# Two-layer MoE trunk: a second home for one down weight, down loads later in the queue, one modulation vector in the arena, and a reordered routing

## What is computed

```python
mod = cs @ w_mod[i] + b_mod[i]
sh_m, sc_m, g_m, sh_f, sc_f, g_f = jnp.split(mod, 6, axis=-1)
...
g_sel = jnp.argmax(g_logits, axis=-1)
p_g = jnp.take_along_axis(g_prob, g_sel[:, None], axis=1)
...
top_val, top_idx = lax.top_k(e_in_group, TOP_K_IN_GROUP)
gate = p_g * jax.nn.softmax(top_val, axis=-1)
...
hg = jnp.einsum('sd,edf->sef', t, w_gate)
hu = jnp.einsum('sd,edf->sef', t, w_up)
act = jax.nn.silu(hg) * hu * combine[:, :, None].astype(t.dtype)
return jnp.einsum('sef,efd->sd', act, w_down)
```

## Time and profile before

| what | value |
|---|---|
| median of three executions | 725.58 us (724.47 to 726.06) |
| profiled execution, its own time | 724.7 us |
| span of that execution | 722.6 us |
| HBM read | 268.16 MB, 373 GB/s over the span |
| TensorE busy | 642.3 us (89%), 4266 matmuls |
| VectorE busy | 365.6 us (51%) |
| ScalarE busy | 173.2 us (24%) |

### The profile page before, as it was taken

The page is one execution under the profiler, slowest core; times in us unless marked ns, Lnnn a source line. Parts: engine busy times, 40 slices in busy tenths (PEclk is TensorE's granted clock), DMA queues, the critical chain, the costliest instruction groups (busy, mean ns, idle before and its releaser), DMA issues.

```text
span 722.6 us, 11521 instructions
## 1 busy us (share of the span) xinstructions
PE 642.3 (89%) x4266; PEld 387.3 (54%) x4266; DVE 365.6 (51%) x894; ACT 173.2 (24%) x368; POOL 24.9 (3%) x54
## 2 busy tenths in 40 slices
PE   2699999999998899898998899999889899889994
PEld 1487667467654454454544457575445554545542
DVE  1259876988354334433344388563443334433345
ACT  2113343032322111221112143232122111221123
POOL 5100400000000000000000000000000000000000
PEclk9999999998999999999999999799999999999998
DMA  8999973995579999999999999987999999999991
GB/s 334 353 405 392 335 294 136 411 421 221 233 290 422 420 422 421 422 423 421 422 422 422 416 397 409 362 339 302 422 421 421 422 422 421 423 423 422 421 382 58
DMA packets 49677, 269.61 MB, mean 373 GB/s; under 512 B 3796, under 2 KB 5908, under 8 KB 25072
## 3 DMA queue, kind: packets, MB, share of 16 engines
q1 hardware_dynamic: 48864, 268.22, 91.7%
q0 software_dynamic: 784, 1.00, 0.5%
HBM read 268.16 MB, written 1.05 MB: 373 GB/s over the span
## 4 chain that ended last, share of the span: by engine, by line
PE 49%; DMA 38%; DVE 5%; SPq 5%; issue 2%; ACT 1%; POOL 0%; POOLq 0%; ACTq 0%; DVEq 0%
DMA ring<-in_w_up 33%; PE bank L902 9%; PE bank L881 9%; PE bank L916 5%; PE bank L758 4%; PE bank L607 4%; DMA early_w<-in_w_in 3%; PE bank L869 2%; PE bank L832 2%; PE bank L682 2%; PE bank L692 2%; PE bank L533 2%; DMA dn_w<-in_w_down 2%; PE bank L647 1%; SPq L350 1%
## 5 line engine op out<-in xcount | busy, mean ns | idle before, releaser
L881 PE MATMUL bank<-ring,arena 128*64 128x256 f32 x1024 | 117.3, 382 | 28.4 <-DMA ring<-in_w_up 28.4
L869 PE MATMUL bank<-ring,arena 128*64 128x256 f32 x1024 | 117.6, 382 | 12.6 <-DMA ring<-in_w_gate 12.6
L1178 ACT CAST xn_parts<-arena 128x512 fp32r<-128x512 f32 x64 | 39.6, 618 | 304.9 <-DVE arena L1652 304.9
L881 PEld LDWEIGHTS bank<-ring,arena 128*64 128x64 f32 x1024 | 71.2, 137 | 73.4 <-DMA ring<-in_w_up 40.2
L902 PE MATMUL bank<-dn_w,hT 128*64 128x512 f32 x480 | 109.5, 598 | 0.8 <-DMA dn_w<-in_w_down 0.8
L869 PEld LDWEIGHTS bank<-ring,arena 128*64 128x64 f32 x1024 | 81.0, 137 | 41.6 <-issue 17.6
L1627 DVE SCALAR_TENSOR_TENSOR hT<-hT,bank 128x256 f32<-128x256 f32 x32 | 19.8, 618 | 119.9 <-PE bank L881 119.9
L916 PE MATMUL bank<-xn_parts,sel 128*128 128x512 f32 x256 | 67.1, 405 | 0.0
L902 PEld LDWEIGHTS bank<-dn_w,hT 128*64 128x64 f32 x480 | 32.0, 136 | 62.6 <-issue 60.7
L1652 DVE SCALAR_TENSOR_TENSOR arena<-bank,hT,gates 128x512 f32<-128x512 f32 x64 | 47.9, 749 | 23.9 <-PE bank L902 23.9
L916 PEld LDWEIGHTS bank<-xn_parts,sel 128*128 128x128 f32 x256 | 45.7, 188 | 21.0 <-issue 12.4
(11 more groups left out here) (287 smaller groups left out, 683.7 us busy)
## 6 DMA issues: line engine op xcount, KB each, us to landing
ring<-in_w_gate SPq DMA_DIRECT2D x32, 2048.0 KB, 13.7
ring<-in_w_up SPq DMA_DIRECT2D x32, 2048.0 KB, 18.1
dn_w<-in_w_down SPq DMA_DIRECT2D x30, 2048.0 KB, 10.3
ring<-in_w_mod SPq DMA_DIRECT2D x21, 2048.0 KB, 18.5
ring<-in_w_in SPq DMA_DIRECT2D x2, 2048.0 KB, 22.7
arena<-in_w_mod SPq DMA_DIRECT2D x2, 2048.0 KB, 19.3
ring<-in_w_down SPq DMA_DIRECT2D x2, 2048.0 KB, 14.5
early_w<-in_w_in SPq DMA_DIRECT2D x1, 2048.0 KB, 21.1
```

The lines of the kernel that those rows point to most:

```text
L869: ins = pe.matmul(bank[2][h * WIN:(h + 1) * WIN, 0:FE], xw[:, b, h, k, :], w[:, h, 0, k, :], start=(k == 0), stop=(k == KT - 1))
L881: ins = pe.matmul(bank[3][h * WIN:(h + 1) * WIN, 0:FE], xw[:, b, h, k, :], w[:, h, 1, k, :], start=(k == 0), stop=(k == KT - 1))
L1178: act.copy(xn_parts[:, 0, b, at], y_s[:, b, at]).then_inc(e["y_hi"], 1)
```

## The change

It has four parts. (1) In layer 0, down(1) gets a room of its own, `second_down`: one expert in `xn`, the other in `gates[:, 2:4]`, in two loads of 1 MB, issued behind down(0). (2) SP's first passes are written out: gate(3) and up(3) stand ahead of the down load, and down loads follow later; the loop is turned so that it issues down(p-2), gate(p), up(p). (3) The vector (1,5) is loaded into the arena, not into ring slots 3 and 2; gate(1) and up(1) of layer 1 no longer wait for chunk 23, and the store of `xgT` does. (4) In the routing the matmuls for the totals come first and into a bank of their own; offsets are added by TensorE in PSUM by accumulation, in place of copies and an add on DVE; the six small operations for the two gates of a token move behind the gather; the turning of these gates into rows (`rows_of((gate1, gate2), 7)`) moves behind the first gate product; in layer 1 only half of (1,5) stands ahead of the totals; in layer 0 three of the eight fold matmuls stand between the two halves of the transposes.

```diff
+        second_down = (xn[:, :, :], gates[:, 2:4, :])
         middle = [(m, slot) for m, slot in zip(halves((1, 2)) + halves((1, 4)) + halves((1, 3)) + halves((1, 5)),
-                                               (1, 0, 3, 2, 0, 1, 3, 2))]
+                                               (1, 0, 3, 2, 0, 1, ARENA_A, ARENA_B))]
...
-                else:
-                    sp.wait_ge(S["chunk_done"], chunk_no["mod", 23] + 1)
                 gate_load(l, 1, 2)
                 up_load(l, 1, 2)
...
                 down(l, 0)
+                if l == 0:
+                    sp.wait_ge(S["reduced"], len(reduced))
+                    for half in range(2):
+                        sp.dma_start(second_down[half].rearrange("p t d -> p (t d)"),
+                                     w_down[l][2 + half].rearrange("(p t) d -> p (t d)", t=FT)).then_inc(second_in, 16)
...
-                with sp.Fori(1, groups) as i:
+                gate_next(2, 0, 4), up_next(2, 0, 4), gate_next(3, 1, 6), up_next(3, 1, 6)
+                if l == 0:
+                    sp.wait_ge(E[l]["down_done"], 2)
+                    down(l, 4)
+                    gate_next(4, 0, 8), up_next(4, 0, 8), gate_next(5, 1, 10), up_next(5, 1, 10), down_next(3, 6)
+                else:
+                    down_next(1, 2)
+                    gate_next(4, 0, 8), down_next(2, 4), up_next(4, 0, 8), gate_next(5, 1, 10), down_next(3, 6), up_next(5, 1, 10)
+                gate_next(6, 0, 12), down_next(4, 8), up_next(6, 0, 12), gate_next(7, 1, 14), down_next(5, 10), up_next(7, 1, 14)
+                with sp.Fori(4, groups) as i:
                     for b in range(2):
+                        e = expert_at(i * XS + (2 * b - 4))
+                        down_next(i * 2 + (b - 2), e)
                         e = expert_at(i * XS + 2 * b)
-                        sp.wait_ge(E[l]["gate_done"], i * 2 + (b - 1))
-                        gate_load(l, b, e)
-                        sp.wait_ge(E[l]["unit_done"], i * 2 + (b - 1))
-                        up_load(l, b, e)
-                        e = expert_at(i * XS + (2 * b - 2))
-                        sp.wait_ge(E[l]["down_done"], i * 4 + (2 * b - 2))
-                        down(l, e)
+                        gate_next(i * 2 + b, b, e)
+                        up_next(i * 2 + b, b, e)
+                sp.wait_ge(E[l]["down_done"], groups * 4 - 4)
+                down(l, NE - 4)
...
+                        if slot_of(n) == ARENA_A:
+                            sp.wait_ge(S["pool_ready"], 4)
                         chunk(n)
...
                 else:
                     fold()
-                    pe.wait_ge(S["col_kept"], columns.index((1, 4)) - 1)
-                    norm_out_row(1, bank[0])
-                    pe.wait_ge(S["row_kept"], 2)
-                    vector((1, 5))
+                    norm_out_row(1, bank[5])
+                    vector((1, 5), (0,))
...
-                rows_of((gate1, gate2), 7)
...
                         gate_half(p, b, i * 16 + 16)
+                        if first:
+                            rows_of((gate1, gate2), 7)
                         up_half(p, b, i * 16 + 16)
-                        if l == 0 and isinstance(p, int) and p == 0:
+                        if first and l == 0:
                             reduce((0, 5))
+                        elif first:
+                            gate((1, 5), 0), gate((1, 5), 1)
...
+                        if l == 0 and n == 2 and isinstance(i, int):
+                            pe.wait_ge(second_in, arrivals(place["out", 0]) + 32)
+                            down(1, second_down)
```

## The result

The changed kernel takes 716.6 us (median of six executions, 713.4 to 720.2) against 725.8 us of the kernel before, run beside it: a ratio of 0.989, with a 95% interval of 0.986 to 0.992. It is faster by 1.1%, by 9 us and not by 16. The profiled execution took 713.5 us, 11.2 less than that of before. In a second comparison the same changed kernel took 714.2 us, ratio 0.984 (0.982 to 0.986). The forecast was 709.6, with a range that ended at 716. Of the times further down one leaves an execution out: in the kernel with no own room in layer 0 it took 1669 us, the eleven others 719 to 727.

What follows compares the result with a forecast made beforehand. Loads, not TensorE, were taken to set the pace of the expert passes. Layer 0's terms summed to -9.7 us and layer 1's to -6.3, together -16.0, for a forecast of 709.6 us, range 703.5 to 716.

Steps and rivals of the forecast that it cites:

- (g): Layer 1, expert passes: new holes in the loads at gate(3), down(2) and down(6), +3.0 us.
- (a): Layer 0, routing: the first gate product comes earlier through less DVE work and gate rows moved behind it, -1.8 us.
- (b): Layer 0: down(1) loads into its own room in the idle 16 us, one load less behind the gap, -5.0 us.
- (c): Layer 0: gate(3) is issued near 195.1, while loads still run, so the standstill closes, -6.3 us.
- (d): Layer 0: new holes of 0.6 us at gate(3), 1.5 at down(4) and 1.3 at down(6), +3.4 us.
- (e): Up to layer 1's first gate product: shorter routing, gate(2) issued at 477.9 instead of 481.93, -4.0 us.
- low-clock rival: Layer 1 routing: second half of (1,5) takes 3.6 us at low clock, (e) only -1.3, time 712.3; 12%.
- (f): Layer 1: gate(3) and up(3) go ahead of down(1), and the standstill from 493.6 closes, -5.3 us.
- down loads come late: Both layers: waits of (g) twice as long, also in layer 0; (c) and (f) together -5.8, time 715.4; 13%.
- other side: TensorE falls to 1.2 GHz in pass 2, 5 or 6 of layer 1; with two such passes 731.6 us; 4%.

Runs made afterwards that it cites:

- TensorE kept busy: Changed kernel with five extra matmuls, results overwritten, ahead of TensorE's wait for down(1) in pass 2 of layer 1: 714.7 us, ratio 0.985.
- (1,5) in the ring: Changed kernel with the vector (1,5) loaded into ring slots 3 and 2 as before, not into the arena: 717.3 us, ratio 0.991.
- routing of before: Changed kernel with the routing undone to that of the kernel before; own room, queue and arena stay: 719.4 us, ratio 0.994.
- layer 1 with the queue of before: Changed kernel with layer 1's load queue behind up(2) in the old order, down(1) ahead of gate(3) and so on: 715.2 us, ratio 0.986.

## Why the prediction was wrong

It forecast -16.0 us and got -9.2 and -11.6. The step that failed is **(g)**: "New holes: 0.4 us at gate(3), 1.3 at down(2), 1.3 at down(6). +3.0", with TensorE waiting 1.0 us in pass 2. Measured were 8.6 to 10 us of lost loading time: 1.5 to 2.7 in the first 20 us, 4.3 at down(2), 2.8 to 3.1 at down(6), and a wait of 3.3 to 3.8 us. What the runs show of it:

- *Loads issued one by one lose rate where one ends and the next begins.* The hand timeline let a load start at full rate if it was issued 1.75 us before the end of the one before. In the trace this costs up to 2.7 us over the first four loads (352 and 378 GB/s), and down(1) lands that much later. One more load in the queue removes it (417 and 421 GB/s), and so does a queue that ends a little later, see the last section. This loss adds to the others and does not make the hole at down(2): that is 3.9 and 4.4 us where the first 20 us lose 0.3 or nothing (TensorE kept busy; (1,5) in the ring).
- *The clock.* The wait of 3.8 us ends in a granted clock of 0.50, that is 1.2 GHz, after it had been 1.00, and the down product is 1.7 us longer (5.35 for 3.65). down(2) waits for that product, and behind the wait of 4.24 us (routing of before) product and hole are both a further 1.0 us longer. So I estimate the clock's share of the hole of 4.3 at 1.7 us, more than half of the 3.0 that are over the forecast. No run shows it by itself.
- *One release depends on the other.* down(2) can only be issued when down(1) has been used, and up(4) stands behind it in SP's queue. By hand this gives a hole of 1.4 us however late down(1) comes: gate(4)'s data end 5.0 - 0.8 = 4.2 us after down(1) lands, and those of down(2) start 3.65 + 1.9 = 5.6 us after it. So the lateness alone does not widen the hole, what lengthens the product does.

The other 1.3 us of the hole at down(2), and the 1.5 to 1.8 that the one at down(6) is over its forecast with the clock at 1.00, no run takes apart. In both places the queue had run empty.

**(a)**, -1.8, was right as a mechanism and depends on the clock. Between down(0) and gate(2) lie 24.3 to 25.0 us with the old routing (three profiles), and with the new one 22.1 in the profiles in which the routing is granted full clock, but 24.6 where it is not (below). **(b)**, -5.0, and **(c)**, -6.3, with **(d)**, +3.4, make -7.9. Taken away from the changed kernel, the room is worth 8.8 us in layer 0, since without it the new order also makes a late down(1). Added to the kernel before, it is worth 3.7, and the later order 2.6 on top, 6.3 together. So what each term is worth depends on what is there already, and the standstill of (c) closes by the room alone, which takes down(1) out from between up(2) and gate(3). (d) by itself was 4.9: 0.6 at gate(3), 2.7 at down(4), where TensorE waited 1.6 to 1.7 us for down(3) and by the forecast not over 0.5, and 1.6 at down(6). Layer 0 as a whole was right in the first profile (-9.7) and is -8.3 on average over the eight profiles with this layer 0 unedited. **(e)**, -4.0, was right: -4.3 in the first profile, -5.2 in the second, and undoing the routing brings back 86.7 us. The second half of (1,5) took 3.27 us instead of 1.9 in the first profile, as the low-clock rival had it, and 1.92 in the nine others that load it into the arena with the new routing. **(f)** was right, the standstill is gone, but by itself that gained nothing (layer 1 with the queue of before).

The terms so measured, -4.3, -5.3 and +10, make +0.4 where layer 1 has -1.9. That adds release times and lost loading time, which are two measures. As lost loading time the kernel before has, by the earlier trace rows, 3.1 us at gate(2) and 4.9 behind up(2), and 2.6 between 460 and 470 (312 GB/s), where gate(1) waits for chunk 23: 10.6 against the 10 of the holes. All of layer 1, from one issue to the other, before and after:

```profile
395.29:689.62 294.33, 268.90 (x1872) 157.97 (x1870) 140.08 (x344) 71.60 (x144) 1.38 (x2) 0.98 0.98 403
385.56:677.99 292.43, 266.94 (x1871) 154.12 (x1872) 140.09 (x342) 71.55 (x145) 1.38 (x2) 0.99 0.99 405
```

That is 12.9 and 11.4 us of lost loading time, a difference of 1.5 for the 1.9 (one GB/s is 0.7 us here), so no other cause is needed.

Of the rivals, "down loads come late" (715.4) is what happened: waits of 3.3 to 3.8 us where 1.0 was forecast, one of 1.6 in layer 0, and a time of 714.2 to 716.6. I had given it 13%, because layer 0 had no such wait by hand. Layer 0 was spared by its room: without it TensorE waits 3.15 us there too. That its 715.4 is so near is in part luck, since it took 3.2 us off (c) and 2.6 off (f), where the two profiles miss 0 and 2.1 us in layer 0, and 4.4 and 2.8 in layer 1. The "other side" had the place of the clock's fall right, pass 2 of layer 1, and its price wrong: 1.7 us of one product, not 11 of a pass, since the clock was back at 0.93 to 1.00 within 4 us. The Trainium skill, "TensorE: Matmul & The Clock Gate", section "HAM oscillation — how this bites in real kernels", has a wait for a DMA of operand data followed each time by a throttled stretch, 1.67 us in its example. The trace agrees on the mechanism; here the product after the wait is 1.7 us longer, which takes a stretch of about twice that at half clock (an estimate).

The version with own rooms in both layers beats both kernels: 708.2 us, ratio 0.978. That is the gain that was forecast, 16.4 us for 16.0, but not in the places: layer 0 gives 7.6 of it where the forecast had 9.7, and layer 1 8.9 where it had 6.3.

## What to carry over

In this kernel the reordered queue paid only once the load that is released last had a room of its own; test the order and the room apart, for here the order was worth nothing without the rooms and 5 us with them, and the rooms 8.9 us without the rest of it. In a timeline, don't let just-in-time loads run back to back for nothing: ask for every load how far before the end of the one ahead it is issued, and where a wait of TensorE is forecast, add what it does to the clock of the next product, and so to the next release. A test that fills a wait must end when the wait would have: here it overran by 1.5 us and hid what it was to show. Count idle time of the loads over the whole layer before and after: several of these edits only moved it.

## Of the hardware, unexpected

*Loads that meet end to end.* In these traces the settled 421 GB/s needed a load issued well ahead. With up(2) issued 4.7 us behind gate(2) (some 2 us before gate(2)'s data end, an estimate) 5 us stretches of the changed kernel ran at 333 to 382 GB/s with a DMA share of 0.94 to 1.00; issued 3.5 us behind, at 428. With the same 4.7 us it depends on how long the loads ahead of gate(2) last. down(0) landed 2.6 us after gate(2)'s issue in the changed kernel, and 2.7 us were lost in the first 20 us; 3.4 us after it in the second profile, and 1.5 were lost; 4.7 us after it with TensorE kept busy, and 0.3 were lost; 6.0 us after it with (1,5) in the ring, and nothing was lost.

*Two levels in the routing of layer 0.* The same code is granted full clock there in some executions, in others not. Busy time from 170 to 186, of the changed kernel:

```profile
170.00:186.00 16.00, 15.76 (x90) 12.71 (x92) 11.82 (x51) 7.35 (x13) 0.00 (x0) 1.00 0.55 209
```

And of the kernel with own rooms, whose code is the same up to there:

```profile
170.00:186.00 16.00, 16.00 (x77) 12.96 (x76) 11.51 (x50) 6.80 (x12) 0.00 (x0) 0.85 0.46 189
```

gate(2) comes 22.1 us behind down(0) in the first and 24.6 in the second. In eight profiles it was four times 22.1 to 22.3, three times 24.6, once 23.1; the granted clock from 170 to 175 us was 1.00 in the four, 0.50 to 0.53 in the three and 0.66 in the one. Both kinds came within one comparison. So a part of the scatter of 1 to 3 us between executions may come from here; that was not tried.
